# The second part of a modulation vector: from TensorE during attention to VectorE during the merge

## The reference

```python
mod = jax.nn.silu(c) @ w_ada[li] + b_ada[li]
sh1, sc1, gt1, sh2, sc2, gt2 = jnp.split(mod[:, None, :], 6, axis=-1)
mod_c = jax.nn.silu(c_ctx) @ w_ada[li] + b_ada[li]
sh1c, sc1c, gt1c, sh2c, sc2c, gt2c = jnp.split(mod_c, 6)
h = modulate(rmsnorm(x, g_pre_mix[li]), sh1, sc1)
hc = modulate(rmsnorm(ctx, g_pre_mix[li]), sh1c, sc1c)
mix, mix_c = token_mixer(h, hc, ...)          # attention, scan, merge
x = x + gt1 * rmsnorm(mix, g_post_mix[li])
h = modulate(rmsnorm(x, g_pre_ffn[li]), sh2, sc2)
...                                           # experts, then gt2
```

## Time and profile before

| | |
|---|---|
| profiled execution | 3802.57 us, its span 3800.8 |
| median of three runs | 3809.71 us |
| TensorE busy | 3484.3 us (92%) |
| VectorE busy | 1575.9 us (41%) |
| ScalarE busy | 1416.8 us (37%) |
| GpSimd busy | 1190.1 us (31%) |
| attention stage | 212 us |
| merge | about 220 us |
| read from HBM | 470.18 MB |

### The profile page before, as it was taken

One profiled execution on the slowest core, in us unless ns is written; L12 is line 12 of the kernel. 1 busy time (PEld: TensorE's weight loads), 2 busy tenths in 40 slices (PEclk: granted clock), 3 DMA queues, 4 the chain that ended last, 5 costly groups with the idle time before them and its releaser, 6 DMA issues.

```text
span 3800.8 us, 43950 instructions
## 1 busy us (share of the span) xinstructions
PE 3484.3 (92%) x17208; PEld 2664.7 (70%) x17208; DVE 1575.9 (41%) x2226; ACT 1416.8 (37%) x1742; POOL 1190.1 (31%) x555
## 2 busy tenths in 40 slices
PE   7999897799959999999638999999899999899999
PEld 4975586578736667666427777777688887678887
DVE  4136525630166666666542332333432132443212
ACT  4225432252235555555133344433432223243221
POOL 2410022634302333333024333322144443334443
PEclk9999998999979999999769999999999999999999
DMA  5322110012227999999623222222032221013222
GB/s 214 102 70 80 66 67 23 1 67 99 89 103 265 348 347 354 366 366 356 268 70 98 69 68 72 73 62 95 23 110 92 99 89 67 23 67 110 93 97 78
DMA packets 94477, 494.51 MB, mean 130 GB/s; under 512 B 21646, under 2 KB 21902, under 8 KB 43760
## 3 DMA queue, kind: packets, MB, share of 16 engines
q1 hardware_dynamic: 74496, 452.75, 33.5%
q0 software_dynamic: 19824, 39.54, 2.9%
HBM read 470.18 MB, written 40.89 MB: 134 GB/s over the span
## 4 chain that ended last, share of the span: by engine, by line
PE 44%; DVE 2%; ACT 2%; issue 1%; POOL 1%; POOLq 0%; DMA 0%; ACTq 0%; DVEq 0%
PE ps L272 10%; PE ps L274 10%; PE ps L273 10%; PE ps L2219 2%; PE ps L2196 2%; PE ps L2174 1%; PE ps L2186 1%; PE ps L2207 1%; PE ps L2175 1%; PE ps L2176 1%; PE ps L2198 1%; PE ps L2848 0%; PE ps L280 0%; PE ps L279 0%; PE ps L278 0%
## 5 line engine op out<-in xcount | busy, mean ns | idle before, releaser
L272 PE MATMUL ps<-arena_r,arena_r 128*128 128x512 f32 x2080 | 842.6, 405 | 39.8 <-POOL ring_r L263 25.0
L273 PE MATMUL ps<-arena_r,arena_r 128*128 128x512 f32 x2080 | 816.0, 392 | 0.0
L263 POOL TENSOR_TENSOR ring_r<-ring,arena_r 128x2048 fp32r<-128x2048 f32 x100 | 466.1, 4662 | 870.8 <-ACT arena_r L259 870.8
L259 ACT ACTIVATE arena_r<-ring 128x2048 fp32r<-128x2048 f32 x166 | 316.6, 1909 | 562.2 <-PE ps L274 408.2
L272 PEld LDWEIGHTS ps<-arena_r,arena_r 128*128 128x128 f32 x2080 | 394.1, 189 | 144.5 <-issue 52.6
L273 PEld LDWEIGHTS ps<-arena_r,arena_r 128*128 128x128 f32 x2080 | 394.7, 190 | 88.5 <-issue 10.6
L263 POOL TENSOR_TENSOR arena_r<-ring,arena_r 128x2048 fp32r<-128x2048 f32 x66 | 304.2, 4609 | 414.2 <-ACT arena_r L259 414.1
L274 PE MATMUL ps<-arena_r,arena_r 128*128 128x512 f32 x1056 | 410.8, 389 | 0.0
L274 PE MATMUL ps<-arena_r,ring_r 128*128 128x512 f32 x1024 | 404.9, 395 | 0.0
L1949 DVE TENSOR_TENSOR arena_r<-arena,arena_r 128x2048 fp32r<-128x2048 f32 x132 | 301.9, 2288 | 168.5 <-ACT arena_r L1907 168.3
L1907 ACT ACTIVATE arena_r<-arena 128x2048 fp32r<-128x2048 f32 x132 | 250.5, 1910 | 125.9 <-DMA arena<-we_gu 102.6
(11 more groups left out here) (392 smaller groups left out, 6017.8 us busy)
## 6 DMA issues: line engine op xcount, KB each, us to landing
ring<-wstream SPq DMA_DIRECT2D x193, 1024.0 KB, 4.9
arena<-we_gu SPq DMA_DIRECT2D x132, 1024.0 KB, 8.2
arena<-we_down SPq DMA_DIRECT2D x66, 1024.0 KB, 7.5
arena<-ys SPq DMA_DIRECT2D x32, 512.0 KB, 8.5
arena<-arena SPq DMA_DIRECT2D x192, 64.0 KB, 2.0
arena<-arena SPq DMA_DIRECT2D x32, 128.0 KB, 4.5
arena<-x_t SPq DMA_DIRECT2D x1, 2048.0 KB, 15.1
h<-arena SPq DMA_DIRECT2D x1, 2048.0 KB, 6.6
```

Source lines behind the costliest of these rows:

```text
L259: act.activation(whalf(c, 0), ring[:, c % NSLOT, :], ACT.Copy).then_inc(sem("chunk_hi"), 1)
L263: pool.tensor_tensor(whalf(c, 1), ring[:, c % NSLOT, :], whalf(c, 0).bitcast(F32), ALU.subtract).then_inc(sem("chunk_lo"), 1)
L272: pe.matmul(out, hi, rhs[0], start=start, stop=False)
L273: pe.matmul(out, hi, rhs[1], start=False, stop=False)
```

## The change

The 16 chunks of the second part leave the ring and stand at the end of `wstream`. In the merge SyncE loads them two at a time (a group, 2 MB, four transfers of 512 KB) into four buffers outside the ring. VectorE forms the group's 4 x 128 columns as partial sums: for each of 8 k-tiles and 2 halves of 256 columns it multiplies the weights by the k-th entry of `cs` (a number per partition) and adds them to the sum before, 16 operations per group. TensorE then sums over the partitions: 4 products with the partial sum (128x128) as the stationary operand and two columns of ones. `mod_vector` stands at the merge's end. Only the column of `c` is formed. The sums are kept where `wdt` and the vector `lam` were, one of the buffers is that of `rope`.

```diff
-CH_MOD = CH_QKV + 12
-CH_XBC = CH_MOD + 4 * D // 256
+CH_XBC = CH_QKV + 12
...
+CH_MOD = CH_END
...
         def mod_vector(dve):
-            dve.wait_ge(sem("mod_turned"), 1)
-            dve.tensor_tensor(mod[:, 16:48, :], split(bank(5, 64, 256), 32, 2),
-                              v("b_ada", 16, 32).unsqueeze(2).to_broadcast([P, 32, 2]), ALU.add).then_inc(sem("mod"), 1)
-            dve.wait_ge(sem("mod"), 1)
+            dve.wait_ge(sem("mod_columns"), 1 + MOD_GROUPS)
+            dve.tensor_tensor(mod[:, 16:48, 0], split(bank(7, 64), 32, 2)[:, :, 0], v("b_ada", 16, 32),
+                              ALU.add).then_inc(sem("mod_used"), 1)
+            dve.wait_ge(sem("mod_used"), 16 * MOD_GROUPS + 1)
...
             def turn(n):
                 if n >= 1:
                     pe.wait_ge(sem("da_turned"), n)
-                    mod_turn(n - 1)
-                c, j = CH_MOD + n // 2, n % 2
-                if j == 0:
-                    arrived(pe, c)
-                for k in range(KT):
-                    mm = pe.matmul(MOD_ROW, cs[:, k, :], wtile(c, k, j), start=(k == 0), stop=(k == KT - 1))
-                if j == 1:
-                    chunk_done(mm)
                 pe.wait_ge(sem("da_diff"), n + 1)
...
-            mod_turn(NU - 1).then_inc(sem("mod_turned"), 1)
...
-                act.activation(MOD_OUT, MOD_ROW, ACT.Copy)
...
+        MOD_GROUPS = 8
+        MOD_HALVES = [view(R + 32768, 4, 256), view(R + 33792, 4, 256), view(R + 17408, 4, 256),
+                      rope[:, :, :].rearrange("p a b -> p (a b)").rearrange("p (a b) -> p a b", b=256)]
+        MOD_SUM = [wdt[:, :, :].rearrange("p a b -> p (a b)"), v("lam")]
+
+        def mod_load(sp, q):
+            if q:
+                sp.wait_ge(sem("mod_used"), 16 * q)
+            for i in range(4):
+                w = wstream[CH_MOD + 2 * q + i // 2][:, i % 2 * 1024:i % 2 * 1024 + 1024]
+                sp.dma_start(MOD_HALVES[i].rearrange("p a b -> p (a b)"), w).then_inc(sem("mod_full"), 16)
+
+        def mod_group_vector(dve, q):
+            dve.wait_ge(sem("mod_full"), 64 * (q + 1))
+            if q:
+                dve.wait_ge(sem("mod_columns"), 1 + q)
+            for k in range(KT):
+                for i in range(2):
+                    w, x = MOD_HALVES[2 * i + k // 4][:, k % 4, :], cs[:, k, 0:1]
+                    if k == 0:
+                        dve.tensor_scalar(MOD_SUM[i], w, x, None, ALU.mult).then_inc(sem("mod_used"), 1)
+                    else:
+                        dve.wait_ge(sem("mod_used"), 16 * q + 2 * k + i - 1)
+                        dve.scalar_tensor_tensor(MOD_SUM[i], w, x, MOD_SUM[i], ALU.mult,
+                                                 ALU.add).then_inc(sem("mod_used"), 1)
+
+        def mod_group_tensor(pe, q):
+            pe.wait_ge(sem("mod_used"), 16 * (q + 1))
+            for m in range(4):
+                mm = pe.matmul(bank(7, 2, 8 * q + 2 * m), MOD_SUM[m // 2][:, m % 2 * P:m % 2 * P + P], C["ones"][:, 0:2],
+                               start=True, stop=True)
+            mm.then_inc(sem("mod_columns"), 1)
@@ merge_tensor, after products(n, ...) @@
                 if n == 0:
                     z_square_sum(pe, 3)
+                elif n % 2 == 0:
+                    mod_group_tensor(pe, n // 2 - 1)
@@ merge_tensor, after products(16 + n, ...) @@
+                if n == 0:
+                    mod_group_tensor(pe, MOD_GROUPS - 1)
@@ merge_vector, after L1501 and L1504 @@
+                if q < 7:
+                    mod_group_vector(dve, q)
             for k in (6, 7):
                 source_lo(dve, 3, k)
+            mod_group_vector(dve, 7)
+            mod_vector(dve)
@@ SyncE's loop, after the ring load @@
+                if last == CH_Z + 2:
+                    mod_load(sp, 0)
+                if CH_MERGE + 2 <= last < CH_MERGE + 16 and (last - CH_MERGE) % 2 == 0:
+                    mod_load(sp, (last - CH_MERGE) // 2)
```

More of the change, by code:

```diff
@@ L92 @@
     "qkv_hi", "qkv_lo", "xbc_hi", "xbc_lo", "source_hi", "source_lo",
-    "mod", "mod_turned", "ada_rows", "ada_turned", "ada_silu", "lam_exp", "lam_dots", "da_bias", "da_diff", "da_exp", "da_head", "da_ln", "da_max", "da_norm", "da_recip", "da_rstd",
+    "mod_used", "mod_full", "ada_rows", "mod_columns", "ada_silu", "lam_exp", "lam_dots", "da_bias", "da_diff", "da_exp", "da_head", "da_ln", "da_max", "da_norm", "da_recip", "da_rstd",
     "da_scores", "da_sq", "da_ss", "da_turn", "da_turned", "da_values", "dt_abs", "dt_diff", "dt_ln",
@@ L385, in ada_tensor @@
                         pe.matmul(bank(6 + m, w), C["ones"], SQ_TOTAL[m], start=True, stop=True).then_inc(sem("st_sums"), 1)
-            turn(1).then_inc(sem("ada_turned"), 1)
+            turn(1).then_inc(sem("mod_columns"), 1)
         def ada_vector(dve):
@@ L412, in ada_vector @@
                     dve.tensor_tensor((HT, HC)[m][:, k, :], x[:, k, :], RSTD[m], ALU.mult).then_inc(sem("st_normed"), 1)
-            dve.wait_ge(sem("ada_turned"), 1)
+            dve.wait_ge(sem("mod_columns"), 1)
             link(dve.tensor_tensor(mod[:, 0:16, :], split(bank(5, 32), 16, 2),
@@ L693, in wT @@
             return view(W0 + 4 * TA + (h % 2) * AT * T, AT, T)
-        MOD_ROW = pf[0:2, 5 * 512 + 384:6 * 512]
-        MOD_OUT = v("lam", 0, P)[0:2, :]
         SC = small[:, 8:40]
@@ L710, in scores @@
                               stop=True).then_inc(sem("da_scores"), 1)
-            def mod_turn(n):
-                return pe.matmul(bank(5, 2, 256 + 2 * n), MOD_OUT, C["ident"][0:2, 0:2], start=True, stop=True)
             def turn(n):
@@ L753, in da_tensor @@
                     square_sum(n // 4 - 1)
-            pe.wait_ge(sem("da_turned"), NU)
-            mod_turn(NU - 1).then_inc(sem("mod_turned"), 1)
             values(H1 - 1)
@@ L794, in da_vector @@
             head(H1 - 1)
-            mod_vector(dve)
         def da_scalar(act):
@@ L3269 @@
     w_ada = chunks(g["w_ada"][0])
-    stream = [w_ada[:8], chunks(w_in[:, :3072]), w_ada[8:], chunks(w_in[:, 4096:6144]), chunks(w_in[:, 3072:4096]),
+    stream = [w_ada[:8], chunks(w_in[:, :3072]), chunks(w_in[:, 4096:6144]), chunks(w_in[:, 3072:4096]),
               chunks(merge), chunks(g["w_out"][0]), chunks(g["w_sh_gate"][0]), chunks(g["w_sh_up"][0]),
@@ L3275 @@
               chunks(b_in[:, 0:2048]), chunks(b_in[:, 2048:3072]), chunks(g["b_w_out_2"][0]),
-              ffn(g["ffn_w_gate_up_2"][1], g["ffn_w_down_2"][1])]
+              ffn(g["ffn_w_gate_up_2"][1], g["ffn_w_down_2"][1]), w_ada[8:]]
     wstream = np.concatenate(stream, axis=0)
-    assert wstream.shape[0] == CH_END
+    assert wstream.shape[0] == CH_MOD + 16
     def row(a):
```

## The result

| | before | after |
|---|---|---|
| median of 6 runs, us | 3810.23 (3798.45 to 3817.74) | 3831.72 (3828.13 to 3838.78) |
| profiled execution, us | 3802.57 | 3828.13 |
| its span, us, and mean granted clock | 3800.8, 0.959 | 3825.9, 0.949 |

The ratio is 1.0066, with a 95% interval of 1.0048 to 1.0083: the change makes the kernel slower by 0.7%. The forecast was 3815 and "no change". The measured time lies in the range of 3798 to 3838, but the likeliest case did not come about, and the stages behave otherwise than the sum had them.

The account below looks back on a forecast made before the run. Plain attention steps were taken as bound by VectorE and ScalarE, value steps as waiting for TensorE. Attention -6.1 and merge +11.3 gave +5.2 on 3802.57, so 3807.8; 7 more for the median made 3815 us, range 3798 to 3838.

Parts of the forecast that it names:

- the likeliest case: Attention 6.1 us shorter and merge 11.3 us longer, 3815 us in all; chance 0.42.
- case 4: Attention: TensorE's clock halves ahead of every value block, each losing 1.7 to 5.2 us, 3838 us in all; chance 0.20.
- two of its own signs: Prediction wrong if plain attention steps fall below 5.1 us, TensorE waits for VectorE's merge sums, or attention clock below 0.8.
- Plain steps bound by VectorE and ScalarE, 5.11 us: Attention steps without value products: VectorE and ScalarE handing over set 5.11 us, so removing TensorE work gains nothing there.
- TensorE's share coming out whole (3752): Attention: as bound by TensorE as its busy share says, so all 68.5 us come out, 3752 us; chance 0.05.
- What the attention would give without the clock, 1.85 per value step: Attention: value products come 1.65 us earlier, the following step loses 0.20; 13.0 us over seven, 13.8 with the stage's end.
- What comes back by the clock, 7.7 us: Attention: half clock on value products costs 1.7 us, half chance for seven heads, certain at head 7; 7.7 us lost.
- Who gets the memory first in the merge: Merge: VectorE's sixteen operations start first and keep GpSimd out until 6.8 or 7.9 us after the group's product starts.
- Late low halves, 2.1 us: Merge: GpSimd's low halves, held up by VectorE's operations, delay TensorE 0.7 us in groups 1, 3 and 5; 2.1 us.
- The small products, 0.9 per group: Merge: TensorE's four small products per group lie on the path, 0.9 us per group, 7.2 us in all.
- Case 3's sum: Merge: GpSimd gets in before or within VectorE's operations, TensorE waits; 14.1 us plus 3 for clock, 3821 us; chance 0.15.
- Transfers: Merge: 3 MB take about 11 us and are wanted after 12.1 to 13.3, so the moved loads are just hidden.

Follow-up runs that it names:

- the filled kernel: The changed kernel with eight products of the old form, read by nobody, in each plain attention step and none in the value steps: 3818.65 us, ratio 1.0033.
- the other execution of this attention: The changed kernel with each group's small products issued one 512-column chunk later in the merge: 3817.41 us, ratio 1.0024.
- without the small products: The kernel before, attention untouched, with the merge's new loads and VectorE operations added but no small products on TensorE: 3808.31 us, ratio 1.0004.
- the kernel without trains: The kernel before, attention untouched, with the merge's new loads and small products on a constant added, but no VectorE group operations: 3820.89 us, ratio 1.0039.

## Where the prediction was right, and where it failed

The measured 3831.72 lies in the stated range, but that is luck and no sign that the sum was right. The sum gave 3815, and "within 0.5%" had a chance of 0.71, while the kernel became 0.66% slower. The part of the range above 3828 had been taken in for case 4, the clock in the attention; what filled it was mostly the merge, which cost 24.4 us where the sum had 11.3. By two of its own signs the prediction comes out wrong or nearly so: TensorE waits for the trains, and the granted clock in the attention is 0.81. Point by point, by its own steps.

- **Plain steps bound by VectorE and ScalarE, 5.11 us.** Right, before and after, to a few tenths. The case of TensorE's share coming out whole (3752) is excluded.
- **What the attention would give without the clock, 1.85 per value step.** A little too high: with the clock up it is 9.35 - 7.75 = 1.60 per step, plus 0.20 in the step behind it. In the loop as a whole the filled kernel gains 11.4 us (190.52 to 179.14), where the sum had 13.0.
- **What comes back by the clock, 7.7 us.** Mis-sized, the first of two failed steps. The mechanism and the places were right. But I gave each of seven heads a half chance of 1.7 us. All seven paid in this execution, 0.13 to 2.8 us against the 7.75 of a full clock, 12.4 us together, so 1.8 each; in the other execution of this attention it is 10.5, with 0.03 to 2.74. The filled kernel gave back 12.3 of the loop (191.41 to 179.14) and 13 of the whole. Head 7, which was to pay 1.7 for certain, took 8.48 us instead of 5.42, so 3.1. It was not case 4 (3.5 per head) either; it ate the gain, to within a few us. The rule that I had cited from the Trainium skill (TensorE: Matmul & The Clock Gate, "HAM oscillation"), that bursts with waits between them re-throttle again and again, points the right way, though the page's own case has longer waits, for DMA, than the 0.52 and 1.14 us between the bursts here. The trace shows the pattern: the granted clock falls to 0.50 to 0.52 once at the loop's start and then once for every head, for 6.8 to 13.7 us each time. I should have drawn the chance from that, and not from the one pair of windows in the earlier trace rows.
- **Who gets the memory first in the merge.** The second failed step. I read one row, the 6.38 of the earlier trace rows, as a rule that a train without gaps keeps GpSimd out to its end (VectorE's stream had not ended there, see above), and set the chance of the other reading at 0.15. In every train of the merge GpSimd came in between two operations or ahead of the first. The page that I weighed against it (the Trainium skill, SBUF — State Buffer, "two separate sides": the pair is locked by the instruction, whichever starts first) describes every one of these rows: the 4.70, the 4.88, and the 4.82 and 7.26 of the experiments.
- **Late low halves, 2.1 us.** Wrong with it: GpSimd never starts late by a train, and without the small products the merge has its old 205.2 us to the tenth.
- **The small products, 0.9 per group.** Right: 0.94 or 0.95 in three kernels.
- **Case 3's sum.** It is the case that came about, with each term too small. Measured per group, with their own 0.95: 2.1 us for even groups (23.87 - 21.76, forecast 1.6) and 3.3 for odd ones (25.05 - 21.76, from the products at 923.12 and 948.17, forecast 2.5), since the operations go every 0.396 us and not every 0.36, and more of the train lies behind GpSimd's. The clock took another 4.9 us in two pairs (28.30 and 26.67 instead of 25.05), and a stretch at 0.52 in the output products some 1.6. TensorE had waited 1.36 and 1.85 us ahead of it, but so it had in the kernel without trains, where the clock held: what decides it stays open here as well. With the first and the last group, 0.98 and 0.94, that makes 24.4, where the case had 17.
- **Transfers.** Right: the rings' loads and the groups' stay ahead; neither the kernel without trains nor the one without small products shows a wait for them in the merge.
- **The sum.** -6.1 + 11.3 = +5.2 was forecast. It was 0 (the merge's first product at the same time to 0.03 us; the attention itself 3.5 longer, which is not clear of its scatter) + 24.4.

## What to carry to other kernels

Taking work off an engine that the profile shows as full pays only where that engine ends last; where a loop is bound by two others, its filling work may be what holds the clock up for the block that comes after, and the cheapest place for extra work is just there (here the plain steps, not the value steps). Place a product that reads another engine's result one stage of work behind the moment when that result is due, not right at it: an interruption of 4.6 us then costs nothing, and here that single choice was worth 16 us of the merge. And when one row of a trace and a rule speak against each other, count how many rows bear on the question before taking the one.

## What was not expected of the hardware

- In the merge VectorE and GpSimd trade SBUF from one instruction to the next. A chain of sixteen short operations lost one place to each low half of GpSimd that fell due within it, and GpSimd's own operation grew by 0.3 us at most. That holds for SCALAR_TENSOR_TENSOR and TENSOR_TENSOR, dependent on each other or not. The low half of the earlier trace rows grew by 1.8 us and is the exception.
- TensorE busy for 2.61 and then 2.26 us of two stretches of 3.40 was followed by 6.8 us at 1.2 GHz, and one idle time of 2.12 us in a stream without other gaps by another 6.8 us. Both fell on the work behind the idle time: the value products, and the small products with the chunk after them. Of three waits of 2.12 us one was followed by 6.8 us of low clock, one by about 3.4 us and one by none.
- Adding a 128x256 row of fp32 to a sum costs VectorE 0.396 us with a per-partition factor and 0.336 without (0.47 and 0.41 in the records, which overlap), also where each operation waits for the one two places before it.
